# Hybrid decoder step on one core: page loads of the sample stage moved out of the prompt's loop, and transposes issued ahead of values

## The reference, cut to what matters

```python
def prompt_layer(x, ...):
    q, kv_c, kv_s, kv_w, gates, u = split_proj(rms_norm(x, g_attn) @ w_in)
    comp = compress_blocks(kv_c, cmp_pe, cmp_w1, cmp_w2)
    ...                     # per 128 queries: three attentions, mixed by gates
    h = merge_and_mlp(x, o, p, w_out, g_mlp, w_up, w_down)

def sample_layer(x, cache_cmp, cache_slc, state_win, state_pool, page_table, ...):
    past_c = cache_cmp[page_table].reshape(B, past, N_KV, 2, HEAD_DIM)
    comp = ...              # compress_blocks of past_c
    phys = page_table[..., jp // BLOCKS_PER_PAGE]
    rows_past = cache_slc[phys[..., None], offs, ...]      # pages of the selected branch
    ...
```

## Time and profile before

| | us |
|---|---|
| median of three runs (range) | 907.37 (906.33 to 907.95) |
| the profiled execution, whole time | 907.63 |
| its span in the trace | 905.8 |
| PE busy | 839.6 (93%) |
| DVE, ACT, POOL busy | 417.6, 335.0, 129.4 |
| compression's block ends, prompt begins | about 213.0 |
| prompt's block ends, sample stage begins | about 307.4 |
| sample stage ends, MLP begins | about 418.9 |

### The profile page before, as it was taken

One profiled execution on the slowest core, in us unless ns is written; L12 is line 12 of the kernel. 1 busy time (PEld: TensorE's weight loads), 2 busy tenths in 40 slices (PEclk: granted clock), 3 DMA queues, 4 the chain that ended last, 5 costly groups with the idle time before them and its releaser, 6 DMA issues.

```text
span 905.8 us, 17118 instructions
## 1 busy us (share of the span) xinstructions
PE 839.6 (93%) x7279; PEld 760.4 (84%) x7279; DVE 417.6 (46%) x776; ACT 335.0 (37%) x618; POOL 129.4 (14%) x157
## 2 busy tenths in 40 slices
PE   5999998997888878897999999999999999999995
PEld 4999977774555645566999999999999999999995
DVE  5435646665555475565327433344333433243432
ACT  6501155553566564454225431043212331043311
POOL 0001101100784325520220000000000000000120
PEclk9999999997999888998999999999999999999998
DMA  8922638832570206517221122222221122222002
GB/s 299 322 72 94 192 84 272 269 119 93 163 205 8 82 1 233 193 61 189 94 94 41 55 91 93 93 93 93 93 84 37 64 93 93 93 94 93 1 1 105
DMA packets 48789, 102.96 MB, mean 114 GB/s; under 512 B 7498, under 2 KB 19166, under 8 KB 46429
## 3 DMA queue, kind: packets, MB, share of 16 engines
q1 hardware_dynamic: 41821, 68.61, 22.9%
q0 software_dynamic: 6912, 33.56, 11.0%
HBM read 97.75 MB, written 8.53 MB: 117 GB/s over the span
## 4 chain that ended last, share of the span: by engine, by line
PE 52%; DVE 1%; ACT 0%; DVEq 0%; issue 0%
PE banks L1981 51%; PE banks L2022 0%; DVE y L1971 0%; PE banks L2048 0%; DVE wl L1901 0%; PE banks L2038 0%; ACT wh L1845 0%; DVE hT L1939 0%; DVE hT L1914 0%; DVE xl L1918 0%; ACT low L1859 0%; DVE xl L1907 0%; ACT xh L1861 0%; DVEq L1794 0%; ACT small L1889 0%
## 5 line engine op out<-in xcount | busy, mean ns | idle before, releaser
L1981 PE MATMUL banks<-xh,wh 128*128 128x288 f32 x640 | 138.0, 297 | 4.3 <-DVE xl L1907 3.9
L1981 PE MATMUL banks<-xl,wh 128*128 128x288 f32 x640 | 137.8, 297 | 0.0
L1981 PE MATMUL banks<-xh,wl 128*128 128x288 f32 x640 | 137.7, 297 | 0.0
L1845 ACT ACTIVATE wh<-low 128x1024 fp32r<-128x1024 f32 x72 | 75.0, 1050 | 103.1 <-PE banks L1981 102.8
L1981 PE MATMUL banks<-ah,wh 128*128 128x288 f32 x512 | 110.1, 297 | 0.0
L1981 PE MATMUL banks<-ah,wl 128*128 128x288 f32 x512 | 109.7, 296 | 0.0
L1981 PE MATMUL banks<-al,wh 128*128 128x288 f32 x512 | 109.6, 296 | 0.0
L1981 PEld LDWEIGHTS banks<-xh,wh 128*128 128x128 f32 x640 | 103.8, 190 | 4.9 <-DVE wl L1901 4.1
L1981 PEld LDWEIGHTS banks<-xh,wl 128*128 128x128 f32 x640 | 103.9, 190 | 0.0
L1981 PEld LDWEIGHTS banks<-xl,wh 128*128 128x128 f32 x640 | 103.9, 190 | 0.0
L1939 DVE TENSOR_TENSOR hT<-banks,hT 128x288 f32<-128x288 f32 x64 | 26.3, 453 | 138.9 <-PE banks L1981 138.9
(11 more groups left out here) (330 smaller groups left out, 1383.2 us busy)
## 6 DMA issues: line engine op xcount, KB each, us to landing
low<-in_w_up SPq DMA_DIRECT2D x8, 2048.0 KB, 7.8
low<-in_w_down SPq DMA_DIRECT2D x8, 2048.0 KB, 7.7
zone<-in_cmp_w SPq DMA_DIRECT2D x16, 256.0 KB
o_swin<-in_state_win SPq DMA_DIRECT2D x8, 504.0 KB
px<-in_x_prompt SPq DMA_DIRECT2D x4, 512.0 KB, 5.3
u_raw<-in_w_in SPq DMA_DIRECT2D x1, 2048.0 KB, 10.0
q_raw<-in_w_in SPq DMA_DIRECT2D x1, 2048.0 KB, 10.3
low<-in_state_win SPq DMA_DIRECT2D x4, 512.0 KB
```

The source lines that it names most:

```text
L1845: act.activation(wcols(m.wh, i), raw_cols(i), ACT.Copy).then_inc(wh_ready, 1)
L1981: last = pe.matmul(out(i, hf), w[wi], half(x[:, k, :], hf), start=first and part == 0, stop=end and part == 2)
```

## The change

Three edits. In `compress`, POOL's queue gets, after the chunks, a wait for the last unit of compression (`hid_done` at 32) and the eight page loads of pair 0. In `prompt`, POOL issues the eight page loads of pair 1 ahead of its loop (behind the memset of `kc2`), and the loads in the loop are gone. In PE's `body`, `turn(j, u + 1)` comes ahead of `values(j, u)`.

```diff
@@ compress, on_gpsimd
             else:
                 pool.wait_ge(blk_turned, CU * (ck - 1))
             load_chunk(pool, m, sems, ck)
+        pool.wait_ge(hid_done, UNITS)
+        for x in range(4):
+            for e in range(2):
+                load_pages(pool, m, 0, e, x, sems)
@@ prompt, gpsimd
             pool.memset(m.kc2, 0.0).then_inc(sems.cleared, 1)
-            loads = [(n, e, x) for n in range(2) for x in range(4) for e in range(2)]
+            for x in range(4):
+                for e in range(2):
+                    load_pages(pool, m, 1, e, x, sems)
             for t in range(HPG * U):
                 pool.wait_ge(scl_ready, t + 1)
...
                 last.then_inc(scaled, 1)
-                if 1 <= t <= len(loads):
-                    n, e, x = loads[t - 1]
-                    load_pages(pool, m, n, e, x, sems)
@@ prompt, tensor
             def body(j, last):
                 for u in range(U):
-                    values(j, u)
                     if not last or u + 1 < U:
                         turn(j, u + 1)
+                    values(j, u)
                     if not last or u + AHEAD < U:
                         scores(j, u + AHEAD)
```

## The result

The changed kernel takes 921.24 us (median of four runs, 918.75 to 923.08), the old one beside it 906.85 us (905.95 to 907.95): a ratio of 1.0148, 95% interval 1.0122 to 1.0174. It is slower, as forecast, but by 14.4 us and not by 4.3, and 4.7 us above the top of the range.

What follows compares the result with a forecast made beforehand. PE at work bounds the end from 419 us, so delays in compression's tail and the prompt move it equally. Terms 5.0 + 1.0 - 1.7 = +4.3 us on the 907.37 median gave 911.7 us, range 907.0 to 916.5.

Steps and rivals of the forecast that it cites:

- loads in compression: issues and DRAIN: Compression's end: POOL's DRAIN waits for the last gather's landing, so the prompt starts later; +5.0 us, bounds +3.9 and +8.2.
- the clock: Prompt's start: PE idles longer and begins at the low clock; +1.0 us, bounds -1.5 and +3.
- loads of pair 1 ahead of POOL's loop: Prompt's start: eight issues fit before POOL's first scaling; cost nothing, up to 1 us if the cover is gone.
- transposes ahead of values: PE's prompt body: waits for ACT's copies stay, gains at the first pass and last pass's end; -1.7 us, bounds 0 and -3.
- the issues cost nothing: Compression's tail: eight gather issues end at 212.9 us, level with DVE's end at 212.79, so alone they cost about nothing.
- its cover: Prompt's start: eight issues keep POOL 9.9 us, its first scaling comes at 11.15 us; they fit by about 1 us.
- The estimate of 3.2 us from the Trainium skill: Compression's end: last gather lands 3.2 us after issue, making the DRAIN term +2.3 us; set aside for the profile's rows.
- Rival A: Compression's end: POOL's DRAIN does not wait for landings; block 1.5 us late, 907.2 us, no change; chance 0.13.
- rival B: PE's prompt body: new order gains all 6.2 us of waits for ACT on top of 1.7; 905.5 us; chance 0.07.
- The 0.3 us that the sum has for the passes: Prompt's passes: a gain of 0.3 us counted within the -1.7 us of the new order.

Runs made afterwards that it cites:

- e2_loads: Old kernel plus both moves of page loads (pair 0 in compression, pair 1 ahead of POOL's loop), old order of PE: 917.69 us, ratio 1.0125.
- e11: Changed kernel, with PE repeating one matmul of the compression tail 24 times to stay busy: ratio 1.0142.
- e6: Old kernel plus 15 POOL memsets in compression's tail and pair 1's gathers ahead of POOL's loop, pair 0's within it: 920.02 us, ratio 1.0109.
- e5: Old kernel, old loop and order, plus 15 POOL memsets in compression's tail in the place of gathers: 915.24 us, ratio 1.0066.
- e8: Old kernel with transposes ahead of values and pair 0's gathers ahead of POOL's loop, pair 1's within it: 911.30 us, ratio 1.0019.
- e12: Old kernel plus 15 POOL memsets in compression's tail and eight more 512 KB direct loads by SP behind its windows: 917.33 us, ratio 1.0088.
- e3: Old kernel with pair 0's eight gathers moved into compression, pair 1's in POOL's loop, old order of PE: 917.42 us, ratio 1.0093.
- e7: Old kernel with four of pair 0's gathers moved into compression, the other twelve in POOL's loop, old order of PE: 912.84 us, ratio 1.0019.
- e1: Old kernel with only PE's new order, transposes ahead of values; all 16 gathers stay in POOL's loop: 907.12 us, ratio 1.0001.
- e9: Changed kernel, with SP's eight window loads at the prompt's start held back until the first reciprocal: 916.08 us, ratio 1.0096.
- e4: Old kernel with pair 0's eight gathers ahead of POOL's loop, pair 1's within it, none in compression: 910.22 us, ratio 1.0002.
- e10: Old kernel with PE's new order and SP's window loads held back until the first reciprocal, old page loads: 908.87 us, ratio 1.0006.

## Why the prediction was wrong in size

Right in sign and in its largest term: POOL's DRAIN waits until its gathers have landed. The terms, as the prediction put them, against what the touched blocks show:

| step | predicted | after |
|---|---|---|
| loads in compression: issues and DRAIN | +5.0 | +7.0 |
| the clock | +1.0 | +1.6 in the prologue, +1.4 in the passes (e2_loads against before) |
| loads of pair 1 ahead of POOL's loop | 0 | **+3.1** |
| transposes ahead of values | -1.7 | -2.5 (the change against e2_loads) |
| sum | +4.3 | +10.6 |

The passes' -1.0 is the sum of two rows here, +1.4 and -2.5, and what POOL's emptier loop gives back, if anything, is in the first of them. The 2.8 us of e11 are more than the 1.6 since they compare with a prologue at the high clock throughout its 32 matmuls, which before didn't have.

**The step that failed is "Loads of pair 1 ahead of POOL's loop. Cost: nothing; if the cover is gone, up to 1 us."** I asked only whether POOL would be back for its first scaling. It was: the last issue ended at 229.83 us and the scaling waited for DVE until 235.20. But its gathers held up the handing over from PE to DVE in the prologue, on the path that sets the start of the first pass. Nothing in the trace of before showed that, since no gathers were in flight there under PE's 32 matmuls; I had bounded the step by its cover and not by a row, where an unknown effect on others would have wanted a wider bound. e6 against e5 gives its price at 3.1 us up to the first scaling (1.6 over the touched blocks, behind a late start), e8 shows it on time and at full clock, and e12 shows that DVE is on time when SP moves as much. The same kind of late signal stands in the tail of compression, where the prediction had the issues cost nothing; the DRAIN hid it.

This step alone would have left the forecast within its range (911.7 + 3.1 = 914.8 us). The miss of 10.1 us is 3.1 from it, 2.0 from the DRAIN, some 2 from the clock less 0.8 from the order, and 3.8 that no term covers (below).

**The DRAIN.** Three small misses on the same side. The first gather started 0.28 us behind the unit's end and two of the issues took 1.05, so the last was issued 9.25 us behind that end and not 8.7. It landed after 6.3 us, where I had taken 5.9. And the DRAIN ended 1.0 us behind the landing; I had set both equal. With the barrier that is 7.0 us, inside my bounds of 3.9 and 8.2. The estimate of 3.2 us from the Trainium skill (DMA: Bandwidth & Descriptors, Anatomy of one DMA) is half of the 6.3 measured: here the trace disagrees. Rival A is out: in e5 the DRAIN ended 1.4 us behind POOL's last instruction, in e2, e3 and the change 6.3 to 6.4 behind it.

**The clock.** In the change it costs 1.6 us in the prologue (PE's 32 matmuls start that much later behind PE's first). I had hoped that 2.4 GHz would come back earlier for it; it did, under the 32 matmuls, and was lost again until 240 us, 21 us behind the memset. With the old order the first pass was 1.4 to 2.9 us longer behind a late start (e2, e3, e5, e12), but not in e6 and e7; with the new order it is even 0.55 shorter than before. By the table the clock comes to 3.0, the upper bound of -1.5 and +3.

**The new order.** The argument was right: the waits for ACT stayed (6.2 before, 7.0 after) and changed sides, so rival B is out. (The 0.3 us that the sum has for the passes followed from no row: the two effects named there, 0.1 us a pass each way, cancel.) On time and alone it is worth 0.8 us (e1): 0.4 in the first pass, where I had 0.33, 0.6 in the last, where I had 1.05, and the middle passes give 0.2 back where I had 0.3 gained. The transposes still wait for ACT's copy in the last pass, 0.90 us at 313.67. Behind a late start it saves more: 2.5 us between e2_loads and the change, 2.0 of it in the first pass.

**What stays open.** The medians differ by 14.4 us, the touched blocks of the two profiled executions by 10.6. The profiled run of the change is its fastest, 2.5 us below its median, that of before 0.8 above; the other 0.5 is in the two outer stretches. Where the change's three slower runs lost their time isn't known, since they have no profile. By the medians of a later measurement the same loads cost 9.7 us in e2_loads, without the new order, and pair 0's alone 9.5 in e3; so a part of the 14.4 may be of the chip or the day. Open too is what holds the signal. PE's row is modelled at its end, as the Trainium skill says (Perfetto Trace Analysis, Tensor Engine Instruction: the profiler "estimates the end time from instruction size + SBUF delay"), so the profile can't tell whether PE finished late or its signal travelled long. One row leans to the former or to a common cause: in compression, with eight gathers being issued, PE's own DRAIN, 3.95 us long, ended at 213.95 us in the change, in the same instant as DVE's delayed copy started (213.93). It was 3.9 to 4.2 us in every run with eight gathers there and 1.5 to 2.2 us in those with four or none.

## What to carry to other kernels

Before moving a DMA that POOL issues to the tail of a block, look at what ends the block: here POOL's DRAIN waited for the landing and 1 us more (6.4 to 7.4 us from the last issue), so such loads are free only where someone else works that long behind them; four instead of eight cost 1.0 us at the seam. A late start had a second price in the clock behind it, not in proportion to the delay: 5.3 us cost another 3.2 in e5, 1.0 us another 1.6 in e7. And hidden issues aren't free by being hidden: gathers issued close together under a chain of PE and DVE hand-overs made one of these up to 3 us late, while those spaced by a scaling did not, and neither did direct loads by SP.

No version here beats the kernel before: the new order alone is level with it (1.0001), and every placement of the gathers outside the loop costs time or gains none.

## What the runs showed that I had not expected

- In the prologue DVE's addition starts 3.0 to 3.4 us behind the end of PE's row when POOL issues eight gathers back to back ahead of its loop (after, e2, e6, e8, e11), 1.5 us with less traffic beside them (e9), and 0.1 when SP moves about as much (e12). In e4 it was 0.4, but DVE's next wait for PE was let go 2.0 us behind PE's row.
- The releaser "remote" stands in DVE's waits, up to the first pass, in eight profiles: all with eight gathers back to back, in compression or ahead of the loop. The six with fewer or none in a row (before, e1, e5, e7, e10, e12) have none.
- Gathers landed 8.8 to 9.6 us from issue beside the windows, and 5.8 to 6.4 in the tail of compression.
- A filler that kept PE busy bought the prologue 2.8 us at 2.4 GHz, and the low clock came afterwards instead, from 234 to 247 us.
